# The last gate chunk and the final norm of a two-block transformer kernel in two halves, and four norms' sums spread by one product with ones

## The chip, the cores and the metric

One NeuronCore of a Trainium2 chip runs the whole kernel in one launch. The metric is the device time in microseconds (us); a time given for a kernel is the median of several executions.

## The reference, cut to what matters

Two transformer blocks over 512 positions of width 1024, in float32. The first has two kinds of attention and a gated feed-forward layer. The second has a pooling mixer, an attention, a second feed-forward layer, and then its last two steps, which are where most of the change lies:

```python
x = x + (silu(h @ w_ffn_gate) * (h @ w_ffn_up)) @ w_ffn_down      # h = rms_norm_2(x, norm_ffn)
gate = sigmoid(rms_norm_2(x, norm_ple) @ w_ple_gate)
x = x + gate * (p @ w_ple_proj)
return rms_norm_2(x, norm_final)

def rms_norm_2(x, gain):
    inv = rsqrt(mean(x * x, axis=-1) + 1e-6)
    return x * inv * gain
```

`rms_norm` of the first block is the same formula.

## The kernel before, in words

Everything is held transposed: `X` has 8 chunks (KD) of 128 features on the partitions, with the 512 positions along the row. A matrix product of one output chunk of 128 features is a *group*: for each of the 8 input chunks three products of 128x128 weights with 128x512 inputs (high part times high part, high times low, low times high), 24 in all, that add up in one bank of the accumulator `ps` (`three`, `group`). Weights come in units of two chunks through three slots. SyncE (SP) loads a unit when the unit three before it is used up (`load`), ScalarE (ACT) rounds it to `w_hi`, VectorE (DVE) subtracts to get `w_lo` (the two functions called `split`). Each engine's order is written out by hand, and an engine that waits for a semaphore holds up all that stands behind it.

**A "late" norm.** Four norms are not applied to a product's input, but to its output: `n_ffn_pre` (before feed-forward ff1), `n_mix2` (before in2), `n_ffn2` (before ff2) and `n_ple` (before the gate, pleg). While the products already run on the unnormed input, ACT squares the 8 chunks of `X` (`square`), GpSimd (POOL) adds the first seven squares into `sqsum` (`sum_squares`, L408), and TensorE (PE) sums `sqsum` and the eighth square over the partitions: `total` has 8 small products, one per 128 positions and source, each of them two instructions of one column (16 in all), and gives 4 sums on each partition. DVE makes the variance of them (`variance`), ACT a guess by Ln and Exp (`guess`), DVE refines it and writes four 128x128 diagonal matrices (`factors`), PE multiplies those with a matrix of ones (`factor`, two instructions of 512 columns), so that all partitions hold the 512 factors, and ACT copies them to `factors_sb` (`late_factors`). From then on DVE scales each group's bank by `factors_sb` as it takes it out (`scaled`, L1226). Banks 0 to 3 take the groups in turn, so that a group waits until the bank's last one has been taken out (`wait_bank`); in ff1 and in2 groups 4 and 5 go to two other banks.

In ff1 and in2 ("wide") the first four groups run interleaved by input chunk (`first_units`), `total` stands ahead of the seventh input chunk and `factor` behind the eighth. In ff2 and pleg only the first two groups are interleaved, `total` follows them, and `factor` follows the next group.

**The end.** pleg has 8 groups. DVE's loop over j takes group j+1 out (`gate_in`, scaled into `hf`), waits for ACT's sigmoid of group j, multiplies by `PP` and adds to `X` (two tensor_tensor). So the additions of chunk 6 stand behind `gate_in(7)`, which waits for the last group. ACT squares each finished chunk for the final norm and POOL adds up. Then, one after the other: `total(n_final)`, `variance`, `guess` (ahead of it a table load, L850), `factors`, `factor`, eight scalar_tensor_tensor from `X` to `OUT` (L1233) and eight stores of 256 KB by SP (L394).

Lines of the helpers, which the trace names: L464 every product, L835 every activation, L1226 tensor_tensor, L1229 and L1230 tensor_scalar, L1233 scalar_tensor_tensor, L404 and L408 POOL's clearing and adding, L375 weight loads.

Of the kernel before, what the change touches and what calls it, by code (L numbers as in the profile page):

```python
# [10 lines left out]
D = 1024  # L11
S = 512
# [75 lines left out]
def build(nc, xT, pT, weights, gains, consts, outT):  # L88
# [10 lines left out]
    with ctx:  # L99
# [105 lines left out]
        with ExitStack() as st:  # L205
# [40 lines left out]
            sem(n) for n in ("silu_ready", "prod_ready", "prod_hi_ready", "prod_lo_ready"))  # L246
        out_ready, out_stored = sem("out_ready"), sem("out_stored")
# [23 lines left out]
        class Norm:  # L271
# [7 lines left out]
            def __init__(self, n, kind, before):  # L279
# [4 lines left out]
                n_f32 = {"split": n, "late": 1, "added": n, "final": 0}[kind]  # L284
                self.factor_used = self.f32(n_f32)
                for e in NORM_EVENTS:
                    norm_counts[e] += (n if e in ("squares", "summed") else n_f32 if e == "f32" else
                                       (n if kind in ("split", "late") else 0) if e in ("hi", "lo") else 1)

        norms = []  # L290
        for n, kind in ((KD, "late"), (4, "split"), (4, "split"), (KD, "added"), (KD, "late"), (KD, "added"),
                        (KD, "late"), (KD, "late"), (KD, "late"), (KD, "final")):
            norms.append(Norm(n, kind, norms[-1] if norms else None))
# [52 lines left out]

        def gcol(name, k):
            c = GAIN_AT[name] + k
            return gain[:, c:c + 1]


        X_PARTS = [(0, 1), (1, 2), (2, 4), (4, 6), (6, 8)]

# [13 lines left out]
        def _(sp):  # L367
# [27 lines left out]
            sp.wait_ge(out_stored, 16 * KD)  # L395
# [3 lines left out]
        def _(pool):  # L399
            def sum_squares(nm):  # L400
# [4 lines left out]
                for j in range(nm.n - 1):  # L405
# [56 lines left out]
        def _(pe):  # L462
# [58 lines left out]
            def total(nm):  # L521
# [8 lines left out]
                last.then_inc(nm.total.sem, 1)  # L530

# [196 lines left out]
            first_units("in2", U_IN2, 2, KS, h_hi, h_lo, parts_of(n_mix2.lo), {KD - 2: lambda: total(n_mix2)})  # L728
            factor(n_mix2)
# [87 lines left out]
            total(n_ple)  # L817
            for u in range(1, 4):
                unit("pleg", U_PLEG + u, 2 * u, 2, KS, h_hi, h_lo, after=lambda j: factor(n_ple) if j == 2 else None)
# [875 lines left out]
```

## Time and profile before

| | |
|---|---|
| time, median of 3 executions | 1394.39 us (1391.86 to 1395.15) |
| the profiled execution: its own time, its span | 1398.8 us, 1396.3 us |
| mean granted TensorE clock | 0.983 of full speed |
| busy share of the span: PE, DVE, ACT, POOL | 96%, 50%, 39%, 10% |
| chain of work that ended last: PE, DVE | 88%, 8% |

Start times in the rows are us from the start of the span. The columns of each view are named with the first group of rows that shows it. Products are pipelined: a row's duration is that of one product, but the next one starts before it ends, so the distance between starts is what one costs.

### The profile page before, as it was taken

Reading aid. Unit: us, or ns where it says so; the run is one execution under the profiler, and the core shown is the slowest. Engines: PE = TensorE matmul, PEld = TensorE weight load, DVE = VectorE, ACT = ScalarE, POOL = GpSimd, SP = SyncE. Lnnn points to the kernel's source line nnn. Section 1 sums busy time; section 2 is a strip of 40 time slices with the busy share of each in tenths; the row PEclk is TensorE's granted clock in tenths of the full one; section 3 lists DMA queues with packets and bytes.
Section 4 is the critical chain, followed back from the end, with each engine's and each line's share of the span. In section 5 each row is a group of like instructions: output and inputs, shape, how many; then the busy total and the mean of one; then the engine's idle time right before and its main releaser. Section 6 shows DMA issues by size and latency. Waiting matters only on the chain.

```text
span 1396.3 us, 14839 instructions
## 1 busy us (share of the span) xinstructions
PE 1341.4 (96%) x6120; PEld 1076.3 (77%) x6120; DVE 691.5 (50%) x922; ACT 544.8 (39%) x736; POOL 144.8 (10%) x132
## 2 busy tenths in 40 slices
PE   7987989999999999998999999999999999999995
PEld 5764658788888888886888888788888888888874
DVE  6998864644453442216434445664444453423254
ACT  6458864532232332224224555542332232322232
POOL 3441002500000000012000001011000000010011
PEclk9999989999999999998999999999999999999997
DMA  6110003122222323231322111223232222232311
GB/s 238 61 60 2 0 1 121 61 77 104 91 91 94 111 69 102 85 113 67 103 93 83 61 61 61 91 91 98 87 111 97 91 91 94 79 104 95 111 61 60
DMA packets 20595, 117.75 MB, mean 84 GB/s; under 512 B 2480, under 2 KB 2864, under 8 KB 9904
## 3 DMA queue, kind: packets, MB, share of 16 engines
q1 hardware_dynamic: 19392, 114.57, 24.0%
q10 hardware_dynamic: 1136, 2.24, 0.4%
q8 instruction: 48, 0.79, 0.2%
q14 instruction: 19, 0.16, 0.0%
HBM read 114.70 MB, written 2.10 MB: 84 GB/s over the span
## 4 chain that ended last, share of the span: by engine, by line
PE 88%; DVE 8%; DMA 1%; ACT 1%; issue 1%; SPq 0%; POOL 0%; POOLq 0%; DVEq 0%
PE ps L464 87%; PE ps L660 2%; DVE rt L1233 1%; DVE w_lo L1226 1%; DMA X<-x_t 1%; DVE nmax L1388 1%; DVE F L1230 1%; DVE X L1226 0%; ACT w_hi L835 0%; DVE rt L1226 0%; DVE ps L1233 0%; DMA w_raw<-weights 0%; DVE OUT L1233 0%; DVE h_lo L1233 0%; DVE y L1226 0%
## 5 line engine op out<-in xcount | busy, mean ns | idle before, releaser
L464 PE MATMUL ps<-h_hi,w_hi 128*128 128x512 f32 x1248 | 497.1, 398 | 19.6 <-DVE w_lo L1226 11.3
L464 PE MATMUL ps<-h_lo,w_hi 128*128 128x512 f32 x1248 | 488.8, 392 | 0.0
L464 PE MATMUL ps<-h_hi,w_lo 128*128 128x512 f32 x1248 | 488.6, 392 | 0.0
L1226 DVE TENSOR_TENSOR w_lo<-w_raw,w_hi 128x2048 fp32r<-128x2048 f32 (+2 forms) x117 | 247.6, 2119 | 276.0 <-ACT w_hi L835 275.9
L464 PEld LDWEIGHTS ps<-h_hi,w_hi 128*128 128x128 f32 x1248 | 236.0, 189 | 78.8 <-issue 14.3
L835 ACT ACTIVATE w_hi<-w_raw 128x2048 fp32r<-128x2048 f32 (+2 forms) x117 | 201.2, 1721 | 196.7 <-DMA w_raw<-weights 196.5
L464 PEld LDWEIGHTS ps<-h_lo,w_hi 128*128 128x128 f32 x1248 | 236.0, 189 | 51.1 <-issue 3.1
L464 PEld LDWEIGHTS ps<-h_hi,w_lo 128*128 128x128 f32 x1248 | 235.9, 189 | 49.7
L408 POOL TENSOR_TENSOR sqsum<-sqsum,sq 128x512 f32<-128x512 f32 x62 | 90.0, 1452 | 901.8 <-ACT sq L835 900.1
L1226 DVE TENSOR_TENSOR hf<-ps,factors_sb 128x512 f32<-128x512 f32 x56 | 38.6, 691 | 199.4 <-PE ps L464 194.3
L464 PE MATMUL ps<-mid_lo,w_hi 128*128 128x512 f32 x352 | 136.9, 389 | 0.0
L464 PE MATMUL ps<-mid_hi,w_hi 128*128 128x512 f32 x352 | 136.9, 389 | 0.0
L464 PE MATMUL ps<-mid_hi,w_lo 128*128 128x512 f32 x352 | 136.9, 389 | 0.0
L835 ACT ACTIVATE mid_hi<-hf 128x512 fp32r<-128x512 f32 x44 | 27.8, 633 | 209.9 <-DVE hf L1226 209.9
L464 PEld LDWEIGHTS ps<-mid_hi,w_hi 128*128 128x128 f32 x352 | 66.1, 188 | 13.8
L464 PEld LDWEIGHTS ps<-mid_hi,w_lo 128*128 128x128 f32 x352 | 66.1, 188 | 13.7
L464 PEld LDWEIGHTS ps<-mid_lo,w_hi 128*128 128x128 f32 x352 | 66.1, 188 | 13.6
L835 ACT ACTIVATE sq<-sq 128x512 f32<-128x512 f32 x44 | 27.7, 632 | 87.9 <-DVE sq L1226 87.9
L660 PEld LDWEIGHTS ps<-ident,F 128*128 128x128 f32 x208 | 23.9, 147 | 42.7 <-DVE F L1230 40.4
L835 ACT ACTIVATE sq<-X 128x512 f32<-128x512 f32 x48 | 30.2, 629 | 64.1 <-DVE X L1226 63.2
L660 PE MATMUL ps<-ident,F 128*128 128x128 f32 x208 | 37.4, 296 | 15.2 <-DVE F L1230 15.2
L1388 DVE TENSOR_REDUCE nmax<-ps 128x1 f32<-128x512 f32 (+2 forms) x64 | 37.5, 587 | 18.0 <-PE ps L464 17.9
(178 smaller groups left out, 1198.1 us busy)
## 6 DMA issues: line engine op xcount, KB each, us to landing
w_raw<-weights SPq DMA_DIRECT2D x81, 1024.0 KB, 4.8
w_raw<-weights SPq DMA_DIRECT2D x32, 704.0 KB, 4.2
out_t<-OUT SPq DMA_DIRECT2D x8, 256.0 KB, 2.0
X<-x_t SPq DMA_DIRECT2D x3, 512.0 KB, 7.4
c<-constants ACTq DMA_DIRECT2D x1, 1280.0 KB, 9.2
w_raw<-weights SPq DMA_DIRECT2D x4, 256.0 KB, 7.6
wp_raw<-weights SPq DMA_DIRECT2D x1, 1024.0 KB, 6.8
X<-x_t SPq DMA_DIRECT2D x2, 256.0 KB, 4.0
```

The costliest lines, as they stand in the source:

```text
L408: nc.gpsimd.tensor_tensor(sqsum[:, :], sqsum[:, :], sq[:, j % 2, :], ALU.add).then_inc(nm.summed.sem, 1)
L464: return nc.tensor.matmul(out, lhsT, rhs, start=start, stop=stop, skip_group_check=loose)
L660: last = nc.tensor.transpose(ps[:, 3 + s % 2, (kb - k0) * P:(kb - k0 + 1) * P], prob[:, s % 3, (kb - k0) * P:(kb - k0 + 1) * P], ident[:, :])
L835: return nc.scalar.activation(out, in_, func, **kw)
L1226: return nc.vector.tensor_tensor(out, a, b, op)
L1230: else nc.vector.tensor_scalar(out, a, s1, None, op0))
L1233: return nc.vector.scalar_tensor_tensor(out=out, in0=a, scalar=s, in1=b, op0=op0, op1=op1)
L1388: nc.vector.tensor_reduce(nmax[:, s:s + 1], ps[:, s % 3, at:end], AX.X, ALU.max, negate=True).then_inc(nmax_ready, 1)
```

## The change

It has two parts.

**Sums spread by one product.** The four late norms get the kind "wide". POOL adds all eight squares (nine events in place of eight), and PE multiplies a 128x128 matrix of ones with `sqsum`: one product of 512 columns (two instructions), after which every partition holds all 512 sums. `total` and `factor` are not called for these norms. DVE and ACT then work on 128x512 tiles: one tensor_scalar out of the bank, Ln and Exp, two tensor_tensor and one scalar_tensor_tensor that writes `factors_sb`. The product stands ahead of the eighth input chunk in ff1 and in2, and in ff2 and pleg three input chunks into group 2.

**The last group and the final norm in halves.** Group 7 of pleg runs as two runs of 24 products of 256 columns, into banks 3 and 6. DVE's loop ends with chunk 6, whose additions no longer stand behind a `gate_in(7)`. Taking out, sigmoid, additions, square, sums, variance, guess, diagonals, the product with ones and the writing of `OUT` are done by halves of 256 positions. Sixteen scalar_tensor_tensor of 256 columns take the place of eight of 512. Six stores take the place of eight; their rows in memory are 1 KB in place of 2 KB, and ACT issues one of them.

The diff, cut to its core:

```diff
+        STORES = [(0, 0, 4), (0, 4, 8), (1, 0, 3), (1, 3, 5), (1, 5, 7), (1, 7, 8)]
...
-            for k in range(KD):
-                sp.wait_ge(out_ready, k + 1)
-                sp.dma_start(outT[k * P:(k + 1) * P, :], OUT[:, k, :]).then_inc(out_stored, 16)
+            for n, (i, k0, k1) in enumerate(STORES):
+                if n != len(STORES) - 2:
+                    sp.wait_ge(out_ready, KD * i + k1)
+                    sp.dma_start(*store(i, k0, k1)).then_inc(out_stored, 16)
...
+            def wide_total(nm):
+                pe.wait_ge(*nm.summed(nm.sums))
+                mm(ps[:, nm.ss_bank, :], ones[:, :], sqsum[:, :]).then_inc(nm.total.sem, 1)
...
                 if wide:
-                    first_units(phase, u_ff, 2, KS, h_hi, h_lo, parts_of(nm.lo), {KD - 2: lambda: total(nm)})
-                    factor(nm)
+                    first_units(phase, u_ff, 2, KS, h_hi, h_lo, parts_of(nm.lo), {KD - 1: lambda: wide_total(nm)})
                 else:
                     first_units(phase, u_ff, 1, KS, h_hi, h_lo, parts_of(nm.lo))
-                    total(nm)
-                    unit(phase, u_ff + 1, 2, 2, KS, h_hi, h_lo, after=lambda j: factor(nm) if j == 2 else None)
+                    unit(phase, u_ff + 1, 2, 2, KS, h_hi, h_lo, hooks={2: {3: lambda: wide_total(nm)}})
...
-            total(n_final)
-            factor(n_final)
+            for i in range(2):
+                bank = ps[:, GATE_BANKS[i], half_of(i)]
+                for k in KS:
+                    t = slice((KD + k) * P, (KD + k + 1) * P)
+                    mm(bank, w_hi[slot][:, t], h_hi[:, k, half_of(i)], k == 0, False)
+                    mm(bank, w_hi[slot][:, t], h_lo[:, k, half_of(i)], False, False)
+                    last = mm(bank, w_lo[slot][:, t], h_hi[:, k, half_of(i)], False, k == KD - 1)
+                last.then_inc(half_done, 1)
+            sums, square = sqsum[:, :], sq[:, 1, :]
+            pe.wait_ge(*n_final.summed(KD))
+            final_part(0, sums)
+            final_part(1, sums)
+            for i in range(2):
+                pe.wait_ge(*n_final.squares(KD + i))
+                final_part(i, square).then_inc(n_final.total.sem, 1)
+            final_factor(0)
+            final_factor(1)
...
+            def wide_guess(nm):
+                act.wait_ge(*nm.var(1))
+                link(af(hf[:, 1, :], hf[:, 0, :], ACT.Ln, scale=-2.0))
+                af(hf[:, 1, :], hf[:, 1, :], ACT.Exp, scale=-0.5).then_inc(nm.guess.sem, 1)
...
+            square(n_final, KD - 2, X[:, KD - 2, :])
+            half_gate(0)
+            half_square(0)
+            half_gate(1)
             tables(LN_EXP)
-            guess(n_final)
+            half_square(1)
+            half_guess(0)
+            half_guess(1)
+            i, k0, k1 = STORES[-2]
+            act.wait_ge(out_ready, KD * i + k1)
+            act.dma_start(*store(i, k0, k1)).then_inc(out_stored, 16)
...
+            def wide_factors(nm):
+                dve.wait_ge(*nm.total(1))
+                ts(hf[:, 0, :], ps[:, nm.ss_bank, :], -0.5 / D, ALU.mult, -0.5 * EPS, ALU.add).then_inc(nm.var.sem, 1)
+                dve.wait_ge(*nm.guess(1))
+                link(tt(hf[:, 0, :], hf[:, 0, :], hf[:, 1, :], ALU.mult))
+                link(tt(hf[:, 0, :], hf[:, 0, :], hf[:, 1, :], ALU.mult))
+                stt(factors_sb[:, :], hf[:, 0, :], 1.5, hf[:, 1, :], ALU.add, ALU.mult).then_inc(nm.f32.sem, 1)
...
-            for j in range(KD):
-                if j + 1 < KD:
+            for j in range(KD - 1):
+                if j + 1 < KD - 1:
                     gate_in(j + 1)
...
+            for i in range(2):
+                half_gate_in(i)
+                half_gate_out(i)
+            half_variance(0)
+            half_variance(1)
+            half_factors(0)
+            half_factors(1)
+            half_apply(0, 0, KD)
+            half_apply(1, 0, KD)
```

The new functions of which only calls are shown do to 256 columns what their namesakes do to 512; `final_part` is two of the small products of `total`, `final_factor` a product of ones with two of the diagonal matrices.

## Rows read from the trace of the kernel before

**Rows 1.** The page: busy time of the engines, and the chain that ended last by engine.
```profile
PE 1341.4 (96%) x6120; PEld 1076.3 (77%) x6120; DVE 691.5 (50%) x922; ACT 544.8 (39%) x736; POOL 144.8 (10%) x132
PE 88%; DVE 8%; DMA 1%; ACT 1%; issue 1%; SPq 0%; POOL 0%; POOLq 0%; DVEq 0%
```

**Rows 2.** Timeline of PE in pleg: start, duration, operation, count, idle before and releaser.
```profile
1339.20 0.39 PE L464 MATMUL ps<-h_hi,w_lo 128*128 128x512 f32 x1
1339.43 0.95 PE L464 MATMUL ps<-ones,sqsum 128*128 128x1 f32 x8
...
1341.13 0.49 PE L464 MATMUL ps<-h_hi,w_hi 128*128 128x512 f32 x1
...
1346.72 1.02 PE L464 MATMUL ps<-diag,ones 128*128 128x512 f32 x2
1347.17 0.80 PE L464 MATMUL ps<-h_hi,w_hi 128*128 128x512 f32 x1
1347.81 0.40 PE L464 MATMUL ps<-h_lo,w_hi 128*128 128x512 f32 x1
...
1353.95 0.50 PE L464 MATMUL ps<-h_hi,w_hi 128*128 128x512 f32 x1 [0.72 <-DVE w_lo L1226]
```

**Rows 3.** Timeline of ACT, then of DVE, in the same stretch.
```profile
1329.08 0.63 ACT L835 ACTIVATE sq<-X 128x512 f32<-128x512 f32 x1 [3.00 <-DVE X L1226]
...
1347.77 0.60 ACT L835 ACTIVATE factors_sb<-ps 128x512 f32<-128x512 f32 x1 [4.53 <-PE ps L464]
...
1348.41 1.29 DVE L1226 TENSOR_TENSOR hf<-ps,factors_sb 128x512 f32<-128x512 f32 x2 [4.96 <-ACT factors_sb L835]
```

**Rows 4.** Timeline of PE in ff2, where group 3 ends and group 4 begins.
```profile
988.54 0.39 PE L464 MATMUL ps<-h_hi,w_lo 128*128 128x512 f32 x1
989.01 0.47 PE L464 MATMUL ps<-h_hi,w_hi 128*128 128x512 f32 x1
```

**Rows 5.** Groups of DVE by form: line, operation, count | busy, mean ns | idle before.
```profile
L1226 DVE TENSOR_TENSOR hf<-ps,factors_sb 128x512 f32<-128x512 f32 x56 | 38.6, 691 | 199.4 <-PE ps L464 194.3 <-ACT factors_sb L835 5.0
...
L1388 DVE TENSOR_REDUCE nmax<-ps 128x1 f32<-128x512 f32 x32 | 21.9, 686 | 6.5 <-PE ps L464 6.5
...
L1388 DVE TENSOR_REDUCE nmax<-ps 128x1 f32<-128x257 f32 x16 | 6.7, 421 | 3.9 <-PE ps L464 3.7
```

**Rows 6.** Timeline of PE in the attention of block 2: products of 128 to 512 columns.
```profile
754.89 1.49 PE L464 MATMUL ps<-E_hi,c 128*128 128x512 f32 x10
756.22 1.56 PE L464 MATMUL ps<-E_lo,c 128*128 128x512 f32 x10
```

**Rows 7.** Weight loads (PEld) by form.
```profile
L464 PEld LDWEIGHTS ps<-h_hi,w_hi 128*128 128x128 f32 x1248 | 236.0, 189 | 78.8 <-issue 14.3 <-DVE h_lo L1233 6.2 <-ACT PP L835 3.8
```

**Rows 8.** Timeline of PE at the end, then the table load of ACT.
```profile
1375.62 0.39 PE L464 MATMUL ps<-h_hi,w_lo 128*128 128x512 f32 x1
1380.56 1.87 PE L464 MATMUL ps<-ones,sqsum 128*128 128x1 f32 x8 [4.56 <-POOL sqsum L408]
...
1386.37 2.08 PE L464 MATMUL ps<-diag,ones 128*128 128x512 f32 x2 [2.23 <-DVE diag L1230]
...
1380.07 1.28 ACT L850 ACT_TABLE_LOAD   x1
```

**Rows 9.** Windows of the end: stretch, length, busy (count) by engine, granted clock, DMA.
```profile
1380.50:1384.20 3.70, 3.57 (x16) 3.49 (x16) 0.03 (x1) 0.85 (x1) 0.01 (x1) 0.50 0.00 0
```

**Rows 10.** Timeline of DVE, and one row of POOL, in the last part of pleg.
```profile
1357.74 1.67 DVE L1226 TENSOR_TENSOR X<-X,hf 128x512 f32<-128x512 f32 x1
...
1388.48 5.36 DVE L1233 SCALAR_TENSOR_TENSOR OUT<-X,gain,ps 128x512 f32<-128x512 f32 x8 [2.17 <-PE ps L464]
...
1357.56 1.30 POOL L408 TENSOR_TENSOR sqsum<-sqsum,sq 128x512 f32<-128x512 f32 x1 [2.52 <-ACT sq L835]
```

**Rows 11.** DMA queues: packets, MB, share of 16 engines; 1380 to 1397, then 630 to 650.
```profile
q1 hardware_dynamic: 1152, 2.10, 31.9%
...
q10 hardware_dynamic: 288, 0.23, 3.6%
```

More of the change, by code:

```diff
@@ L352, in build, with store @@
         X_PARTS = [(0, 1), (1, 2), (2, 4), (4, 6), (6, 8)]
+        STORES = [(0, 0, 4), (0, 4, 8), (1, 0, 3), (1, 3, 5), (1, 5, 7), (1, 7, 8)]
+        def store(i, k0, k1):
+            return (outT[k0 * P:k1 * P, half_of(i)].rearrange("(k p) s -> p k s", p=P), OUT[:, k0:k1, half_of(i)])
         def landed(u):
@@ L404, in sum_squares @@
                 nc.gpsimd.memset(sqsum[:, :], 0.0).then_inc(nm.summed.sem, 1)
-                for j in range(nm.n - 1):
+                for j in range(nm.sums - 1):
                     pool.wait_ge(*nm.squares(j + 1))
@@ L726, in vee @@
                 last.then_inc(v2tr_done, 1)
[L728 to L729 removed]
+            first_units("in2", U_IN2, 2, KS, h_hi, h_lo, parts_of(n_mix2.lo), {KD - 1: lambda: wide_total(n_mix2)})
             for u in range(2, 8):
@@ L816, in _, with final_part, final_factor @@
             first_units("pleg", U_PLEG, 1, KS, h_hi, h_lo, parts_of(n_ple.lo))
-            total(n_ple)
             for u in range(1, 4):
-                unit("pleg", U_PLEG + u, 2 * u, 2, KS, h_hi, h_lo, after=lambda j: factor(n_ple) if j == 2 else None)
-            total(n_final)
-            factor(n_final)
+                unit("pleg", U_PLEG + u, 2 * u, 2 if u < 3 else 1, KS, h_hi, h_lo,
+                     hooks={2: {3: lambda: wide_total(n_ple)}})
+            def final_part(i, src):
+                for b in (2 * i, 2 * i + 1):
+                    last = mm(ps[:, SUM_BANKS[i], b:b + 1], src[:, b * P:(b + 1) * P], ones[:, 0:1],
+                              src is sums and b == 2 * i, True, loose=True)
+                return last
+            def final_factor(i):
+                pe.wait_ge(*n_final.diag(i + 1))
+                mm(ps[:, FACTOR_BANKS[i], 0:HALF], ones[:, :], diag[:, 2 * i:2 * i + 2, :]).then_inc(n_final.factor.sem, 1)
+            slot = (U_PLEG + 3) % SLOTS
+            wait_bank("pleg", 7)
+            pe.wait_ge(evac_dve, EVAC["pleg", 4][1])
+            for i in range(2):
[15 more added lines that the diff above has]
+            final_factor(1)
         @block.scalar
@@ L1425, in ffn @@
             def ffn(phase, u_ff, mids0, nm, wide):
-                variance(nm)
-                factors(nm)
-                dve.wait_ge(*nm.f32(1))
+                wide_factors(nm)
                 for i in range(KF // 2):
@@ L1456, in _ @@
             apply_post(n_ffn_post, F, "norm_ffn_post", KD, n_mix2, "norm_mix_2", U_IN2 + 2)
-            variance(n_mix2)
-            factors(n_mix2)
+            wide_factors(n_mix2)
             def chunk2(j):
@@ L1566, in _ @@
             late_low(n_ple, "norm_ple_2", KD - 1)
-            variance(n_ple)
-            factors(n_ple)
-            dve.wait_ge(*n_ple.f32(1))
+            wide_factors(n_ple)
             def gate_in(j):
@@ L1583, in _, with half_gate_in @@
                 tt(X[:, j, :], X[:, j, :], hf[:, j % 2, :], ALU.add).then_inc(x_new[1], 1)
+            gate_in(0)
+            for j in range(KD - 1):
+                if j + 1 < KD - 1:
+                    gate_in(j + 1)
+                gate_out(j)
                 if j < 4 and j % 2 == 0:
                     split(U_PLEG + j // 2 + 2)
-            variance(n_final)
-            factors(n_final)
-            dve.wait_ge(*n_final.factor(1))
-            for k in range(KD):
-                stt(OUT[:, k, :], X[:, k, :], gcol("norm_final_2", k), ps[:, R_BANK, :], ALU.mult, ALU.mult
-                    ).then_inc(out_ready, 1)
+            def half_gate_in(i):
+                dve.wait_ge(half_done, i + 1)
+                tt(hf[:, 1, half_of(i)], ps[:, GATE_BANKS[i], half_of(i)], factors_sb[:, half_of(i)], ALU.mult
+                   ).then_inc(half_in, 1)
@@ new lines, in half_factors, with half_apply @@
+            def half_factors(i):
+                b = slice(2 * i, 2 * i + 2)
+                dve.wait_ge(*n_final.guess(i + 1))
+                link(refine(stat[:, 3, b], stat[:, 0, b], stat[:, 2, b]))
+                for c in (2 * i, 2 * i + 1):
+                    last = ts(diag[:, c, :], ident[:, :], stat[:, 3, c:c + 1], ALU.mult)
+                last.then_inc(n_final.diag.sem, 1)
+            def half_apply(i, k0, k1):
+                dve.wait_ge(*n_final.factor(i + 1))
+                for k in range(k0, k1):
+                    stt(OUT[:, k, half_of(i)], X[:, k, half_of(i)], gcol("norm_final_2", k),
+                        ps[:, FACTOR_BANKS[i], 0:HALF], ALU.mult, ALU.mult).then_inc(out_ready, 1)
```

66 lines of the change are left out of this document (43 added, 23 removed).

## The prediction

> **What bounds the kernel now.** I read the page first: PE is busy for 96% of the span and holds 88% of the chain that ended last [rows 1]. So away from the end a change is worth what it takes off PE's own queue, or off a wait of PE. The timeline of PE through one late norm, in pleg, shows what the norm costs there: the sixteen small products begin at 1339.43 and the next ordinary product at 1341.13, and between 1346.72 and 1347.81 the factor product stands with one ordinary one [rows 2]. Then the timelines of ACT and DVE: the first group is taken out at 1348.41, as soon as ACT has copied the factors [rows 3], and PE waits 0.72 us ahead of group 4, since the weights' low part stands on DVE and ACT behind that take-out [rows 2]. Last the end: PE's last group ends at 1376.01 (1375.62 + 0.39), and the remaining 20.3 us of the span are one chain that passes from engine to engine, in which PE works at the 0.50 granted clock, its 1.2 GHz level [rows 8, 9].
>
> **The norms' sums.** Removed on PE, per norm: the small products, 1341.13 - 1339.43 = 1.70 us, and the factor product. An ordinary product costs 0.23 (1339.20 to 1339.43), so the factor product costs 1347.81 - 1346.72 - 0.23 = 0.86 [rows 2]. Added: one product of ones with 512 columns, the same shape, 0.86. What is left is 1.70 us per norm.
> - ff1 and in2: PE runs without a wait around the norm, and the gain is PE's: 1.70 each, 3.40.
> - ff2: 1.70, and group 4 no longer waits for its bank. That wait is 989.01 - 988.54 - 0.23 = 0.24 [rows 4]. 1.94.
> - pleg: here the chain to the first take-out counts, since PE waits for what stands behind it. Before, it takes from 1339.43 to 1348.41, 8.98 us. After: nine products of group 2 (9 x 0.23 = 2.07), the product up to its result (1.05, as from 1346.72 to ACT's 1347.77 [rows 2, 3]), one DVE step of 512 columns (0.69 [rows 5]), Ln and Exp (2 x 0.63 [rows 3]), three DVE steps (3 x 0.69), 0.1 for handing over: 7.24. The take-out comes 1.74 earlier, PE itself is 1.70 earlier, so the wait of 0.72 stays and the gain is 1.70.
>
> Sum 3.40 + 1.94 + 1.70 = **7.0 us**. The five wide steps of DVE and ACT and POOL's eighth addition cost nothing in ff1, in2 and ff2: two to four groups of 24 x 0.23 = 5.5 us each cover them. Without that cover they would cost what they cost in pleg.
>
> The added wait: PE's queue now waits inside a group for POOL's last addition, and all products stand behind it. In pleg the last square starts at 1329.08 [rows 3] and POOL needs 1.30 for an addition [rows 10], so the sum is there before 1332; PE comes to it at 1341.5. In ff1, in2 and ff2 the squares also end groups ahead of the product. On DVE the first take-out, on ACT the table load and the next weights' split wait behind the chain; all are earlier than before. SP's load of the small weight tile in in2 waits for the norm's sum, which comes up to 12 products (2.8 us) later, but it stands behind a load that waits for PE's first group anyway: nothing.
>
> **The end, on the axis of the profile.** First the half products. Whole ones cost 0.23, half of it is 0.115. The nearest row is a run of ten products with 2560 columns in 756.22 - 754.89 = 1.33 us, 0.133 for a mean of 256 columns, but with four of 128 in it [rows 6]. I take 0.115: 48 x 0.115 = 5.5, as the whole group, with a bound of 48 x 0.133 = 6.4, 0.9 more. So half 1 ends at 1376.0.
> - DVE's take-out, sigmoid, table load, square of half 1. A step of 256 columns: 257 in place of 512 columns save 686 - 421 = 265 ns [rows 5], so 0.69 becomes 0.43; I take 0.43 for ACT too. The table load is 1.28 [rows 8] and covers the two additions. 3 x 0.43 + 1.28 = 2.57: 1378.6. Half 0's additions stand ahead on DVE and may meet POOL's last addition: one of 512 columns took 1.67 in place of 0.69 when POOL had begun 0.18 earlier [rows 10]. Between 0 and 1.0; I take the middle, 0.5: 1379.1. That the additions of chunk 6 no longer wait for the last group, and POOL with them, is what makes the sum of seven squares ready by then.
> - The sums: four small instructions are left in this place, at 1.87 / 8 = 0.23 each [rows 8], 0.9; at the full clock (0.95 / 8 [rows 2]) 0.5. I take 0.9, as the engine has little to do between: 1380.0.
> - Variance to diagonals: DVE writes both halves' diagonals before it applies anything, so the 2.23 of before stays [rows 8]: 1382.2. The first half's product with ones, 2.08 / 2, runs beside half 1's diagonals; 0.1 is left. 1382.3.
> - Sixteen steps of 256 columns: 5.36 / 8 - 0.265 = 0.405 each [rows 5, 10], 6.5 in place of 5.4: 1388.8.
> - From the last step to the end 1396.3 - (1388.48 + 5.36) = 2.46, kept; a smaller last store may save 0.3, more stores in rows of 1 KB may cost 0.3.
>
> DVE's last step ends at 1388.8 in place of 1393.84: **5.0 us**. Bounds: best 5.0 + 0.5 + 0.4 + 0.3 = 6.2; worst 5.0 - 0.5 - 0.9 - 0.3 = 3.3. ACT's own store is its last instruction and holds up nothing.
>
> The row of 257 columns shows 421 ns where half of 686 would be 343 [rows 5]. A rule speaks against halves here: the Trainium skill, "VectorE: DVE Perf Modes", section "The TRN2 errata — SBUF-src ops pay a fixed extra latency per instruction", says that a vector instruction pays a fixed latency however small it is, and advises tiles of 512 elements or more; by its formula for float32, an estimate, 256 elements take (256 + 151) / 0.96 = 424 ns. The trace agrees with that. With 424 ns for each of the sixteen steps the sum would be 0.3 us longer, 1382.7.
>
> Total 7.0 + 5.0 = 12.0. The durations are those of one execution (1398.8 us, of which the span is 1396.3), 4.4 us above the median of the runs. None of the steps scales with that, so I take 12.0 from the median: 1394.39 - 12.0 = **1382.4 us**.
>
> **The rivals.**
> - *Weight loads show under half products.* Each product has a load of 189 ns [rows 7]; under 512 columns it is hidden, since 0.23 is all that a pair costs [rows 2]. If a half product can't hide it, 48 x (0.189 - 0.115) = 3.6 us are lost: 1386.0. For: the load is longer than 0.115. Against: ten products with ten loads in 1.33 us [rows 6], less than 189 ns each. A rule of the Trainium skill ("TensorE: Matmul & The Clock Gate", "Part 3: Packing small matmuls — row/col tiling") would have it so, as it lets a load overlap a running product only in another group of rows; the rows of whole products disagree.
> - *The wide chain decides in ff2 and pleg.* If the five steps of 512 columns take 1.7 us longer than I add up, the gain there goes: 12.0 - 3.6 = 8.4, 1386.0. For: pleg has no slack, PE waits there before and after. Against: all its steps have rows.
> - *The end gives nothing.* More instructions with a fixed part, DVE and POOL in each other's way, half 0's factors behind half 1's variance in DVE's order, so that the halves hardly overlap (the change would then not do what it says): 1394.39 - 7.0 = 1387.4. With the rival above: 1391.0, within 0.3%.
> - *Slower: stores in rows of 1 KB.* 2.10 MB become 2048 rows, 128 per DMA engine. The first store can go four steps after 1382.3, at 1383.9, less the 7.0 of the norms: 1376.9. The end is not earlier than before if 128 rows take over 1396.3 - 2.46 - 1376.9 = 16.9 us, so from 132 ns a row. Before, a packet takes 0.319 x 16 x 17 us / 1152 = 75 ns; those of 0.8 KB on average at 630 to 650 take 0.036 x 16 x 20 / 288 = 40 ns [rows 11]. At 180 ns the time would be 1400.5. It needs more than twice a 2 KB row for 1 KB.
>
> **How the numbers follow.** Forecast 0.61; loads shown 0.08; wide chain 0.12; end gives nothing 0.10; both of these 0.05; stores 0.04. A measurement of this kernel can tell about 0.3%, 4.2 us, from no change: faster 0.61 + 0.08 + 0.12 + 0.10 = 0.91, same 0.05, slower 0.04. The forecast's own bounds are 1381.2 to 1384.1, and with the runs' half spread of 1.65 some 1379.5 to 1385.8; the first two rivals lie at 1386.0. From 1379 to 1387 holds these three, 0.81.
>
> **What would show it.** In the changed profile: one pair of products `ones, sqsum` of 512 columns per norm and 1.7 us less between the products around it; no idle of PE in ff2, 0.7 ahead of pleg's group 4; half products 0.115 apart; the table load between sigmoid and square of half 1; `OUT` steps 0.4 apart, the first some 6.3 us after PE's last gate product; the last store landing 2.5 after the last step. Wrong would be: PE waiting at the product with ones, half products 0.19 apart, or DMA still busy long after DVE's last step.

## The result and the profile after

The changed kernel takes 1383.18 us (median of 5 executions, 1382.63 to 1386.45) against 1394.39 for the kernel before on the same chip: a ratio of 0.9919 [0.9899, 0.9938], 11.2 us less. The prediction was 1382.4 in a range of 1379 to 1387. The profiled execution took 1383.08 with a span of 1381.4, 14.9 us under the span of before; why that is more than the medians differ by is told below.

**The sums.** PE's timeline in pleg after the change, which answers to [rows 2]:

```profile
1332.18 0.39 PE L481 MATMUL ps<-h_hi,w_lo 128*128 128x512 f32 x1
1332.40 1.02 PE L481 MATMUL ps<-sqsum,ones 128*128 128x512 f32 x2
1332.86 0.80 PE L481 MATMUL ps<-h_hi,w_hi 128*128 128x512 f32 x1
1333.50 0.40 PE L481 MATMUL ps<-h_lo,w_hi 128*128 128x512 f32 x1
...
1343.24 0.50 PE L481 MATMUL ps<-h_hi,w_hi 128*128 128x512 f32 x1 [0.93 <-DVE w_lo L1297]
1343.58 0.39 PE L481 MATMUL ps<-h_lo,w_hi 128*128 128x512 f32 x1
```

The sixteen small products and the factor product are gone. One pair of 512 columns stands in their place, and it costs 1333.50 - 1332.40 - 0.23 = 0.87 us, what the factor product cost (0.86). The products run through without a wait for the sum, and PE still waits ahead of group 4 for the weights' low part, 0.93 in place of 0.72. What follows in the chain is seen in DVE's timeline, with two rows of ACT's behind it (they answer to [rows 3]):

```profile
1333.46 0.69 DVE L1300 TENSOR_SCALAR hf<-ps 128x512 f32<-128x512 f32 x1 [10.85 <-PE ps L481]
1335.52 1.42 DVE L1297 TENSOR_TENSOR hf<-hf 128x512 f32<-128x512 f32 x2 [1.36 <-ACT hf L883]
1336.97 0.69 DVE L1304 SCALAR_TENSOR_TENSOR factors_sb<-hf 128x512 f32<-128x512 f32 x1
1337.70 1.29 DVE L1297 TENSOR_TENSOR hf<-ps,factors_sb 128x512 f32<-128x512 f32 x2
...
1334.19 1.30 ACT L883 ACTIVATE hf<-hf 128x512 f32<-128x512 f32 x2 [12.89 <-DVE hf L1300]
1335.50 1.28 ACT L898 ACT_TABLE_LOAD   x1
```

From PE's pair to the first take-out 1337.70 - 1332.40 = 5.30 us pass. The take-out comes 1348.41 - 1337.70 = 10.71 before that of [rows 3].

How far each product stands ahead of the same product of before, stage by stage, tells where the gain arose. In ff1 I take the last product ahead of `total` in the kernel before and the second one behind its factor product; 25 others lie between these two in either kernel. The timeline of PE in ff1, before:

```profile
291.68 0.39 PE L464 MATMUL ps<-h_hi,w_lo 128*128 128x512 f32 x1
291.91 0.28 PE L464 MATMUL ps<-ones,sqsum 128*128 128x1 f32 x2
...
299.20 1.02 PE L464 MATMUL ps<-diag,ones 128*128 128x512 f32 x2
299.65 0.80 PE L464 MATMUL ps<-h_hi,w_hi 128*128 128x512 f32 x1
300.29 0.40 PE L464 MATMUL ps<-h_lo,w_hi 128*128 128x512 f32 x1
```

and the same two products and what stands between them, after:

```profile
287.74 0.39 PE L481 MATMUL ps<-h_hi,w_lo 128*128 128x512 f32 x1
...
290.69 1.02 PE L481 MATMUL ps<-sqsum,ones 128*128 128x512 f32 x2
...
294.54 0.39 PE L481 MATMUL ps<-h_lo,w_hi 128*128 128x512 f32 x1
```

300.29 - 291.68 = 8.61 became 294.54 - 287.74 = 6.80: **1.81** us. The same reading gives, over the whole trace:

| up to | ahead of before, us | of it new |
|---|---|---|
| start of ff1 | 1.5 | 1.5, ahead of any edit |
| ff1, ahead of the norm | 3.9 | 2.4, clock |
| ff1, behind the norm | 5.7 | 1.8, norm |
| in2, behind the norm | 6.6 | -1.0, clock; 1.8, norm |
| ff2, behind group 4 | 8.8 | 2.2, norm and the bank's wait |
| pleg, ahead of the norm | 9.1 | 0.3, weights that landed sooner |
| pleg, group 4 | 10.7 | 1.6, norm |
| end | 14.9 | 4.2 |

The norms gave 1.8, 1.8, 2.2 and 1.6, which is 7.5 before rounding, and the end 4.2, 11.7 in all. The other 3.2 lie where the two kernels are the same. (In in2 the granted clock fell sooner and came back later in the changed kernel's profile than in that of before.) Windows over the start of ff1 (stretch, length, busy and count by engine, granted clock, DMA) show the largest of them, before:

```profile
273.00:276.00 3.00, 2.25 (x5) 1.39 (x6) 2.97 (x6) 2.37 (x5) 1.51 (x2) 0.57 0.00 0
276.00:280.00 4.00, 4.00 (x11) 3.03 (x11) 2.77 (x4) 3.19 (x4) 1.28 (x1) 0.50 0.01 4
```

and after:

```profile
273.00:276.00 3.00, 2.45 (x11) 2.03 (x12) 2.93 (x6) 1.87 (x5) 2.05 (x2) 1.00 0.02 5
276.00:280.00 4.00, 4.00 (x19) 3.33 (x18) 2.82 (x3) 2.92 (x3) 1.30 (x1) 1.00 0.00 0
```

At 0.50, the 1.2 GHz level, eleven products ran in four microseconds, at 1.00 nineteen. So the profiles differ by 14.9, and the medians by 11.2, near the 11.7 that the edits account for.

**The end.** PE's timeline from the first half product on, which answers to [rows 8]:

```profile
1359.70 0.28 PE L481 MATMUL ps<-h_hi,w_hi 128*128 128x256 f32 x1
...
1365.33 0.28 PE L481 MATMUL ps<-h_hi,w_lo 128*128 128x256 f32 x1
1365.88 1.05 PE L481 MATMUL ps<-ones,sqsum 128*128 128x1 f32 x8 [0.28 <-POOL sqsum L425]
1366.80 0.58 PE L481 MATMUL ps<-ones,sq 128*128 128x1 f32 x4
1368.68 1.01 PE L481 MATMUL ps<-ones,sq 128*128 128x1 f32 x4 [1.29 <-ACT sq L883]
1370.92 2.20 PE L481 MATMUL ps<-diag,ones 128*128 128x256 f32 x4 [1.23 <-DVE diag L1301]
```

The 48 half products lie 5.63 / 47 = 0.12 apart. PE's wait for POOL, 4.56 us before, is 0.28; the wait for the diagonals, 2.23, is 1.23, since the first half's product goes while DVE writes the second half's. On DVE, POOL and ACT, one after the other (for [rows 10] and the table load of [rows 8]):

```profile
1364.72 1.39 DVE L1297 TENSOR_TENSOR X<-X,hf 128x256 f32<-128x256 f32 x1
1366.03 0.41 DVE L1297 TENSOR_TENSOR hf<-ps,factors_sb 128x256 f32<-128x256 f32 x1
...
1372.18 6.36 DVE L1304 SCALAR_TENSOR_TENSOR OUT<-X,gain,ps 128x256 f32<-128x256 f32 x16 [0.33 <-PE ps L481]
...
1362.66 3.17 POOL L425 TENSOR_TENSOR sqsum<-sqsum,sq 128x512 f32<-128x512 f32 x2 [3.96 <-ACT sq L883]
...
1366.91 1.28 ACT L898 ACT_TABLE_LOAD   x1
1368.21 0.42 ACT L883 ACTIVATE sq<-X 128x256 f32<-128x256 f32 x1
```

Half 0's addition takes 1.39 where that of half 1 takes 0.42; half 1's square waits for ACT's table load. The scaling starts at 1372.18 and ends at 1378.54, and the span ends 2.8 later, at 1381.35. Windows of one microsecond (the last two figures are the DMA engines' busy share and GB/s) say what binds there:

```profile
1373.00:1374.00 1.00, 0.12 (x1) 0.00 (x0) 1.00 (x4) 0.00 (x0) 0.00 (x0) 0.50 0.00 0
1374.00:1375.00 1.00, 0.00 (x0) 0.00 (x0) 1.00 (x4) 0.00 (x0) 0.00 (x0) 0.50 0.18 65
1375.00:1376.00 1.00, 0.00 (x0) 0.00 (x0) 1.00 (x4) 0.00 (x0) 0.00 (x0) 0.50 1.08 385
1376.00:1377.00 1.00, 0.00 (x0) 0.00 (x0) 1.00 (x4) 0.00 (x0) 0.00 (x0) 0.50 0.87 307
...
1379.00:1380.00 1.00, 0.00 (x0) 0.00 (x0) 0.00 (x0) 0.00 (x0) 0.00 (x0) 0.50 1.09 385
```

The DMA engines stand idle until 1374.8, for the first store waits for four steps. From then on they move 382 to 387 GB/s in each whole window up to 1380, but for 307 in that from 1376 to 1377.

### The profile page after: what moved, and what is told of

Read it like the earlier page. It is cut to its first block, busy times and chain, and to the rows that moved or that the text cites. A ratio compares the mean times of both kernels' runs of the same rounds, so it can differ in the third digit from the quotient of the medians.

```text
span 1381.4 us, 14763 instructions
## 1 busy us (share of the span) xinstructions
PE 1329.6 (96%) x6082; PEld 1067.1 (77%) x6082; DVE 701.1 (51%) x921; ACT 546.1 (40%) x736; POOL 149.5 (11%) x136
## 4 chain that ended last, share of the span: by engine, by line
PE 87%; DVE 9%; DMA 1%; ACT 1%; issue 1%; POOL 0%; SPq 0%; DVEq 0%; POOLq 0%
PE ps L481 86%; PE ps L682 2%; DMA w_raw<-weights 1%; DVE rt L1304 1%; DVE w_lo L1297 1%; DVE nmax L1469 1%; DVE F L1301 1%; DVE X L1297 1%; ACT w_hi L883 1%; DVE OUT L1304 0%; DVE rt L1297 0%; DVE hf L1297 0%; DVE ps L1304 0%; POOL sqsum L425 0%; DVE h_lo L1304 0%
## 5 line engine op out<-in xcount | busy, mean ns | idle before, releaser
L481 PE MATMUL ps<-h_hi,w_hi 128*128 128x512 f32 (+1 forms) x1256 | 497.1, 396 | 20.1 <-DVE w_lo L1297 11.7
L481 PE MATMUL ps<-h_lo,w_hi 128*128 128x512 f32 (+1 forms) x1256 | 489.1, 389 | 0.0
L481 PE MATMUL ps<-h_hi,w_lo 128*128 128x512 f32 (+1 forms) x1256 | 488.9, 389 | 0.0
L481 PEld LDWEIGHTS ps<-h_hi,w_hi 128*128 128x128 f32 x1256 | 236.9, 189 | 78.3 <-issue 14.1
L425 POOL TENSOR_TENSOR sqsum<-sqsum,sq 128x512 f32<-128x512 f32 x66 | 94.8, 1436 | 910.0 <-ACT sq L883 908.2
L1297 DVE TENSOR_TENSOR hf<-ps,factors_sb 128x512 f32<-128x512 f32 (+1 forms) x57 | 38.7, 681 | 190.5 <-PE ps L481 190.4
L481 PEld LDWEIGHTS ps<-mid_lo,w_hi 128*128 128x128 f32 x352 | 66.1, 188 | 13.8
L481 PEld LDWEIGHTS ps<-mid_hi,w_hi 128*128 128x128 f32 x352 | 66.1, 188 | 13.8
L883 ACT ACTIVATE sq<-X 128x512 f32<-128x512 f32 (+1 forms) x49 | 30.4, 620 | 68.2 <-DVE X L1297 67.2
```

The source lines that it names most:

```text
L425: nc.gpsimd.tensor_tensor(sqsum[:, :], sqsum[:, :], sq[:, j % 2, :], ALU.add).then_inc(nm.summed.sem, 1)
L481: return nc.tensor.matmul(out, lhsT, rhs, start=start, stop=stop, skip_group_check=loose)
L883: return nc.scalar.activation(out, in_, func, **kw)
L1297: return nc.vector.tensor_tensor(out, a, b, op)
```

## The experiments

The measure of the end is the **stretch** from the start of PE's last gate product to the end of the span, from the trace's own times: 20.7 before, 16.0 after. Of this difference of 4.7, 0.4 is no gain, since the last half product starts 0.4 later than a whole one would (48 halves take 0.3 longer than 24 whole ones, and the last half starts 0.1 closer to the end). That leaves the 4.2 of the table. The changed kernel, run twice more as it is, gave 1384.72 us, 0.9918 [0.99, 0.9935], and 1383.81 us, 0.993 [0.9916, 0.9944], so the medians of equal kernels differ by up to 1.5 us; the stretch was 16.0 in all three profiles. One thing can move it: the granted clock under PE's small sums, by 0.3 to 0.4 in two cases below. Ratios are to the kernel before on the same chip.

**1. The parts, each alone.** The first run has the four wide norms and before's end (all hunks of the end undone, of which one stands here):

```diff
-                unit("pleg", U_PLEG + u, 2 * u, 2 if u < 3 else 1, KS, h_hi, h_lo,
-                     hooks={2: {3: lambda: wide_total(n_ple)}})
...
+                unit("pleg", U_PLEG + u, 2 * u, 2, KS, h_hi, h_lo, hooks={2: {3: lambda: wide_total(n_ple)}})
+            total(n_final)
+            factor(n_final)
```

The second has the end in halves and before's norms (the start of its diff); the third is the changed kernel again.

```diff
-        for n, kind in ((KD, "late"), (4, "split"), (4, "split"), (KD, "added"), (KD, "wide"), (KD, "added"),
-                        (KD, "wide"), (KD, "wide"), (KD, "wide"), (KD, "final")):
+        for n, kind in ((KD, "late"), (4, "split"), (4, "split"), (KD, "added"), (KD, "late"), (KD, "added"),
+                        (KD, "late"), (KD, "late"), (KD, "late"), (KD, "final")):
...
```

> The four wide norms alone, with the end as before. If the norms' sums give what the prediction added up (7.0 us, 7.6 by the shifts read from the two traces), the time is about 1387 us, ratio 0.995, and the stretch from PE's last gate product to the end of the span stays 20.7 us. If the gain came from the end alone, or from the chance differences between the two profiled executions (1.5 us ahead of ff1, 2.4 us of half clock at the start of ff1), it stays within 2 us of before.

> The halves at the end alone, with the four norms as before. If the end gives 4 to 5 us by itself, the time is about 1390 us, ratio 0.997, and the stretch from PE's last gate product to the end of the span is 16.1 us as in the changed kernel. If the end gains only together with the norms, the stretch is over 18 us.

> The changed kernel itself, on the chip of the others: ratio 0.992, stretch from PE's last gate product to the end 16.1 us. If the half clock at the start of ff1 or in2 comes and goes by chance, its profile may show it in another place than before.

The norms alone took 1389.54 us, 0.9945 [0.9927, 0.9964], which is 7.7 us less (5.0 to 10.2), with a stretch of 20.4. The end alone took 1391.77 us, 0.9966 [0.9952, 0.998], 4.7 us less (2.8 to 6.7), with a stretch of 16.0. The two ratios make 0.9911 together, and the changed kernel has 0.9918. The traces say the same more sharply: read as in the table, the run of the norms alone has 1.8, 1.8, 2.2 and 1.6 at the four norms, 7.5 in all, and the run of the end alone has 0.0 there. So the parts don't disturb each other, and each is as large as the trace of the changed kernel says. That the stretch of the norms alone is 0.3 under the 20.7 of before is mostly the clock: its first eight small sums took 1.61 at a mean granted clock of 0.60, those of before 1.87 at 0.50 [rows 8, 9].

**2. Order or halves.** The end has two changes in one: additions and squares of chunk 6 are no longer behind the last group, and the last group's own chain runs in halves. This run has wide norms and before's end, with only DVE's order moved.

```diff
-                if j + 1 < KD:
+                if j + 1 < KD - 1:
                     gate_in(j + 1)
+                if j == KD - 1:
+                    gate_in(j)
```

> The wide norms, and at the end no halves at all: only DVE's order is changed, so that the additions of chunk 6 stand ahead of taking out group 7. Theory A, that halving makes the end's gain: the stretch from PE's last gate product to the end falls only by the 0.45 us by which POOL was later than the eighth square, to 20.2 us, time 1386.7. Theory B, that the order makes most of it, since POOL's last addition, the first eight small products and the last chunk's additions all come earlier: stretch 17.5 to 18.2 us, time 1384 to 1385.

The run took 1386.54 us, 0.9931 [0.9915, 0.9948], and its stretch of 18.7 lies between the two theories. The rows of DVE, POOL, PE and ACT in this run say why:

```profile
1369.13 1.65 DVE L1241 TENSOR_TENSOR X<-X,hf 128x512 f32<-128x512 f32 x1
...
1368.97 1.26 POOL L424 TENSOR_TENSOR sqsum<-sqsum,sq 128x512 f32<-128x512 f32 x1 [2.90 <-ACT sq L852]
...
1370.28 1.05 PE L480 MATMUL ps<-ones,sqsum 128*128 128x1 f32 x8 [3.30 <-POOL sqsum L424]
...
1368.28 0.61 ACT L852 ACTIVATE sq<-X 128x512 f32<-128x512 f32 x1
```

DVE had added chunk 6 in time, but ACT squared it only behind the last group's sigmoid. So POOL's addition still came late, and held DVE's addition and PE's sums. A second run moved ACT's square too:

```diff
+                if j == KD - 1:
+                    act.wait_ge(x_new[1], j)
+                    square(n_final, j - 1, X[:, j - 1, :])
                 act.wait_ge(evac_dve, EVAC["pleg", j][1])
...
-                if j:
+                if 0 < j < KD - 1:
```

> As the run with the order alone (wide norms, whole last group, whole end, DVE adds chunk 6 before it takes group 7 out), and ACT squares chunk 6 ahead of the sigmoid of group 7 too, as the changed kernel does. Theory A (the part of the end's gain that the order alone doesn't give is the halves' own): POOL's last addition is already free of the chain there, and the stretch from the start of PE's last gate product to the end stays at 18.7 within 0.3. Theory B (the order alone was only half done, since ACT's square of chunk 6 stood behind the last sigmoid, at 1368.28, so that POOL's addition came at 1368.97, clashed with DVE's last addition, 1.65 in place of 0.69, and held PE's sums): POOL is done before PE's last product ends, DVE's last addition falls to 0.7, and the stretch comes to 17.5 to 17.9, so that the order on both engines gives some 2.8 us of the end's gain and the halves 1.6 to 1.8.

The run took 1386.5 us, 0.9932 [0.9915, 0.9949]; its stretch, 1365.52 to 1383.4, is 17.9, the upper edge of B. PE's wait for POOL shrinks and DVE's addition takes its usual 0.69 again, in PE's and DVE's timelines:

```profile
1366.48 1.05 PE L480 MATMUL ps<-ones,sqsum 128*128 128x1 f32 x8 [0.57 <-POOL sqsum L424]
...
1368.06 0.69 DVE L1244 TENSOR_TENSOR X<-X,hf 128x512 f32<-128x512 f32 x1
```

So of the end's gain of 4.2 the order on both engines is worth 20.37 - 17.93 = 2.4 us, all that is done in halves 17.93 - 16.02 - 0.42 = 1.5, and the 0.3 that is left is mostly the clock under before's small sums. Theory B had put the order at 2.8, since it counted from 20.7.

**3. What of the halves counts.** Four edits of the changed kernel. *Whole last group*: 24 products of 512 columns, then halves as before.

```diff
-            for i in range(2):
-                bank = ps[:, GATE_BANKS[i], half_of(i)]
+            bank = ps[:, GATE_BANKS[0], :]
...
-                last.then_inc(half_done, 1)
+            last.then_inc(half_done, 2)
```

> The changed kernel, but gate group 7 is 24 products of 512 columns in one bank again, and both halves of the rest start behind its last one; all else is in halves. Theory A (what halving the products gives is that half 0's take-out, sigmoid and addition lie beside half 1's products): PE's products take as long as before (24 at about 0.23, 5.5 us, against 5.75 for 48 halves), half 0's 2.5 us of work come behind them, and the stretch from the start of the last product to the end grows from 16.0 by 1.2 to 2.2 us. Theory B (half 1's chain behind the table load sets the end, and half 0 only waits for it): it grows by under 0.6 us.

The run took 1385.74 us, 0.9936 [0.9922, 0.9949]; its stretch, 1366.97 to 1384.4, is 17.5 and 1.4 longer, theory A. Its last product starts 0.4 sooner, though: from the wide product to the last product it is 32.5 us, where the changed kernel has 32.9. So half products, which let half 0's steps run beside PE, are worth 1.0 net.

*Whole scaling*: both factor products into one bank, eight steps of 512 columns, eight stores of 2 KB rows.

```diff
-            half_apply(0, 0, KD)
-            half_apply(1, 0, KD)
+            dve.wait_ge(*n_final.factor(2))
+            for k in range(KD):
+                stt(OUT[:, k, :], X[:, k, :], gcol("norm_final_2", k), ps[:, FACTOR_BANKS[0], :], ALU.mult, ALU.mult
+                    ).then_inc(out_ready, 1)
...
```

> The changed kernel, but the two factor products write the halves of one bank and the last scaling runs over 512 positions: 8 steps and 8 stores of 2 KB rows, as before the change. Theory A (the halves of the output are worth nothing: the transfers bind the stretch behind the last scaling in either form, 9.22 us from its start to the end with halves, 7.82 without): the scaling starts about 1.0 later, behind the second half's product, and ends as far behind its start as in the kernel before, so the span stays within 0.5 us of the changed kernel's 1381.4 to 1382.2. Theory B (the early start of the first half's stores is what the end gains): the stretch from the start of PE's last half product to the end, 16.0 to 16.1 us with halves, grows by over 1.0 us. Time by A: 1383 to 1385, by B: 1386 and more.

The run took 1384.52 us, 0.993 [0.9918, 0.9942]; its stretch, 1365.79 to 1381.4, is 15.6 and 0.4 shorter. So the output in halves, with its six stores, gains nothing and costs 0.4. The scaling starts 1.0 later, at 1373.61, but takes 5.36 in place of 6.36, and its stores go after one step each, so that the transfers start 9.5 behind the last half product in both kernels (DVE's timeline, then windows):

```profile
1373.61 5.36 DVE L1301 SCALAR_TENSOR_TENSOR OUT<-X,gain,ps 128x512 f32<-128x512 f32 x8 [1.31 <-PE ps L480]
...
1375.00:1376.00 1.00, 0.00 (x0) 0.00 (x0) 1.00 (x3) 0.00 (x0) 0.00 (x0) 0.50 0.75 291
1376.00:1377.00 1.00, 0.00 (x0) 0.00 (x0) 1.00 (x3) 0.00 (x0) 0.00 (x0) 0.50 1.05 408
```

*Ten finer stores*: the first after one step.

```diff
-        STORES = [(0, 0, 4), (0, 4, 8), (1, 0, 3), (1, 3, 5), (1, 5, 7), (1, 7, 8)]
+        STORES = [(0, 0, 1), (0, 1, 2), (0, 2, 4), (0, 4, 6), (0, 6, 8), (1, 0, 2), (1, 2, 4), (1, 4, 6), (1, 6, 7), (1, 7, 8)]
```

> The changed kernel with ten stores instead of six: the first two of one chunk of 128 rows each, the rest of two, the last two of one. Theory A (the transfers bind the end and start too late: the first of the six stores waits for four scaling steps, 1.7 us): the DMA queues start about 1.2 us sooner behind the first step, the end comes 0.4 to 1.0 us sooner, the stretch from PE's last half product 15.0 to 15.6. Theory B (the stores run as fast as the scaling steps come, and ten issues cost more than six): no change within 0.3 us, or up to 0.5 us later.

The run took 1382.72 us, 0.9918 [0.9904, 0.9932]; its stretch, 1362.97 to 1378.6, is 15.65 and 0.4 shorter, just short of theory A's range. That is as much as whole scaling gave, with the halves kept. So it isn't shown that the halves themselves cost anything: the run before changed steps, rows and stores at once, and finer stores alone win the 0.4 too. The scaling of this run starts at 1369.81, and DMA is busy from 1371 on, though not full, since the sixteen steps now set the pace:

```profile
1371.00:1372.00 1.00, 0.00 (x0) 0.00 (x0) 1.00 (x4) 0.00 (x0) 0.00 (x0) 0.50 0.70 247
1372.00:1373.00 1.00, 0.00 (x0) 0.00 (x0) 1.00 (x4) 0.00 (x0) 0.00 (x0) 0.50 0.66 234
```

*PE sums the seventh square itself*, four products more and one addition of POOL less.

```diff
-            pe.wait_ge(*n_final.summed(KD))
-            final_part(0, sums)
-            final_part(1, sums)
+            pe.wait_ge(*n_final.summed(KD - 1))
+            pe.wait_ge(*n_final.squares(KD - 1))
+            for src in (sums, seventh):
+                final_part(0, src)
+                final_part(1, src)
```

> The changed kernel, but PE takes the seventh square into the sums itself with four more products, and POOL's last addition is gone. Theory A (POOL's addition of 3.17 for two holds DVE's first half addition, 1.39 instead of about 0.43, and PE's sums, 0.28): the first half addition comes down to 0.4 to 0.5, the sums start without a wait on POOL, and the stretch from PE's last half product to the end falls from 16.0 by 0.5 to 0.9 us, the time to about 1384. Theory B (the stretch is set from half 1's chain, behind the table load and its square, and by the stores): the addition gets shorter, and the end doesn't move (16.0 within 0.2).

The run took 1384.28 us, 0.9928 [0.9915, 0.9941]; its stretch, 1365.82 to 1381.5, is 15.65 and 0.4 shorter, between the two theories. POOL's clash is real, as DVE's and then POOL's timeline of this run show:

```profile
1365.20 0.43 DVE L1299 TENSOR_TENSOR X<-X,hf 128x256 f32<-128x256 f32 x1
...
1363.14 1.74 POOL L425 TENSOR_TENSOR sqsum<-sqsum,sq 128x512 f32<-128x512 f32 x1 [3.96 <-ACT sq L885]
```

The addition fell from 1.39 to 0.43, but only 0.4 of that reached the end; half 1's take-out then waits for PE, and its square for the table load. The medians of these four can't be told from the changed kernel's; their stretches, of one profile each, are what the verdicts rest on. The last four small sums took 1.01 to 1.02 us in all four, as in the changed kernel, so the clock has no part in these differences.

**4. The wait in pleg, and all together.** *Early splitting*: ACT and DVE split the weights of groups 4 and 5 before the norm's wide chain, while they wait for PE's sum.

```diff
+            split(U_PLEG + 2)
             wide_guess(n_ple)
...
-                if j < 4 and j % 2 == 0:
-                    split(U_PLEG + j // 2 + 2)
+                if j == 2:
+                    split(U_PLEG + 3)
```

> The changed kernel, but ACT and DVE split the weights of gate groups 4 and 5 into high and low parts ahead of the gate norm's wide chain, in the time in which they wait for PE's sum, instead of behind the first gate chunk. Theory A (with the gate norm shorter, the low half of those weights is now what PE's group 4 waits for, 0.93 us): the wait goes, PE starts group 4 behind group 3 without a gap, and all that follows is 0.9 sooner; ACT's 1.90 and DVE's 2.29 us of splitting no longer stand between the first gate chunks either. The stretch from the wide sum's product (1332.40) to the start of the last half product (1365.33), 32.9 us, comes to 32.0. Theory B (another wait takes its place, the bank that DVE takes out late): it stays over 32.6.

The run took 1382.08 us, 0.9917 [0.9903, 0.9931]. From the wide product at 1333.03 to the last half product at 1364.72 it is 31.7 us in place of 32.9, theory A. The 1.2 is more than the 0.93 of the wait: a product else starts 0.16 before the one ahead of it ends (0.39 long, 0.23 apart), and the second one behind the idle time started 0.34 later and not 0.23 (1343.24 and 1343.58 after the change). The stretch fell too, from 16.0 to 15.6, and that is the clock: the last four small sums took 0.61 us at a granted clock of 1.00, where the changed kernel's three profiles have 1.01 at 0.50. Whether the splitting has a part in that isn't shown. DVE's row has moved into the time in which it stood idle (a row of PE with the four sums behind it):

```profile
1325.18 2.29 DVE L1298 TENSOR_TENSOR w_lo<-w_raw,w_hi 128x2048 fp32r<-128x2048 f32 x1 [1.98 <-ACT w_hi L883]
...
1368.08 0.61 PE L481 MATMUL ps<-ones,sq 128*128 128x1 f32 x4 [1.29 <-ACT sq L883]
```

*All that helped*: early splitting; PE's seventh square; half 0 summed, refined and spread first; half 1's square on DVE; three chunks scaled in halves and five whole; nine stores. The core of it:

```diff
+            tt(sq[:, 1, h], X[:, KD - 1, h], X[:, KD - 1, h], ALU.mult).then_inc(n_final.squares.sem, 1)
             half_variance(0)
...
+            half_apply(0, 0, LEAD)
+            dve.wait_ge(*n_final.factor(2))
+            for k in range(LEAD, KD):
+                stt(OUT[:, k, :] ... ps[:, 0:5:4, 0:HALF], ALU.mult, ALU.mult).then_inc(out_ready, 1)
+            half_apply(1, 0, LEAD)
```

> All that the runs so far found, together: the early splitting; PE sums the seventh square; half 0 is summed first and its factors are made ahead of half 1's; DVE squares half 1 itself, so that it doesn't wait behind ACT's table load; the first three chunks are scaled in halves of 256 (half 0 first, half 1 last) and the other five over 512 positions, with nine smaller stores. Theory A (the links add up): 0.9 from the splitting; scaling starts 5.8 behind the start of the last half product instead of 6.85, takes 5.75 instead of 6.36, and the last store lands 2.4 behind it: a stretch of 14.0 instead of 16.0; in all 2.5 to 3.0 under the changed kernel on the same chip, a ratio to the kernel before of about 0.990. Theory B (the stores bind the stretch whatever starts them, 2.10 MB at 390 to 400 GB/s): the stretch doesn't come under 15.3, in all 1.5 or less.

> The changed kernel as it is, on the same chip as the two others: a ratio of 0.992 within 0.001, and a stretch of 16.0 to 16.1 us from the start of the last half product to the end.

The first of these two runs took 1380.02 us, 0.9902 [0.9886, 0.9917], against 1383.81 for the changed kernel on the same chip: 3.8 us less, somewhat more than A's 2.5 to 3.0. The stretch, 1366.18 to 1380.0, is 13.8 (A: 14.0), and 1334.49 to 1366.18 is 31.7 as in the run before, so the two profiles account for 2.2 + 1.2 = 3.4. DVE's scaling starts 5.6 behind the start of the last half product; the transfers start 1.4 behind that, and from 1374 to 1377 they run at 388 to 406 GB/s:

```profile
1371.78 5.74 DVE L1310 SCALAR_TENSOR_TENSOR OUT<-X,gain,ps 128x256 f32<-128x256 f32 x11
...
1374.00:1375.00 1.00, 0.00 (x0) 0.00 (x0) 1.00 (x3) 0.00 (x0) 0.00 (x0) 0.50 1.07 388
1375.00:1376.00 1.00, 0.00 (x0) 0.00 (x0) 1.00 (x3) 0.00 (x0) 0.00 (x0) 0.50 1.05 406
```

This version is faster than the kernel before, and by its median and its stretch faster than the changed one, though the intervals of these two ratios just touch.

## Why the prediction was right, point by point

- **The total, 12.0; measured 11.2 by the medians (8.6 to 14.1) and 11.7 by the trace.** That it came so near is in part luck: the sums gave 0.5 more than added up and the end 0.8 less, and the interval of the medians is wider than either.
- **The sums, 7.0; measured 7.5 in the trace and in that of the norms alone.** One pair of 512 columns costs what the factor product cost (0.87 against 0.86), as put. ff1 and in2 gave 1.8 each where 1.70 was added up, ff2 2.2 where it was 1.94, pleg 1.6 where it was 1.70. The 0.1 more in ff1 and in2 can be read behind the small products of before: the first ordinary product there takes 0.49 [rows 2], and in ff2 the next one starts 0.33 behind it (976.83 and 977.16), not 0.23.
- **pleg's wait** was to stay at 0.7 and became 0.93: the chain to the first take-out is 5.30 from the pair (forecast 1.05 + 0.69 + 1.26 + 2.07 + 0.1 = 5.17), and PE comes there 0.1 sooner than put. The wait was real time, as the early splitting shows.
- **The wide chain hidden in ff1, in2 and ff2**: PE has no wait there. The rival that it decides is out.
- **The added wait of PE for POOL's eighth addition**: none shows.
- **The end, 5.0; measured 4.2.** This is the term that was mis-sized. Half products: 48 x 0.12 = 5.75, not 5.5, 0.3 lost. From the last half product's end (1365.61) to the end of scaling 12.93 where 12.8 was added up: POOL's clash cost half 1's take-out 0.42, near the 0.5 put down, and the sixteen steps took 6.36, not 6.5. Behind the last step 2.8 and not 2.46, another 0.4: the forecast kept before's tail because it put the last step at the head of the chain. The windows show the transfers there instead: the stream of 2.10 MB starts 2.6 us into the scaling and runs at 382 to 387 GB/s, but for one window, up to 1380; finer stores took these 0.4 away. 0.3 + 0.13 + 0.4 = 0.8, the difference.
- **What made the end gain** was argued as halves and, in one sentence, as order. The runs show order 2.4 and halves 1.5. Of the halves the products are worth 1.0 net; scaling in halves, which the forecast counted on to start the last part early, gave nothing, and with six stores it lost 0.4.
- **Weight loads under half products**: the loads take 192 ns each, the products follow 0.12 apart all the same, so they are hidden here. The rule of the Trainium skill that was weighed ("TensorE: Matmul & The Clock Gate", "Part 3: Packing small matmuls — row/col tiling") does not describe these rows. PEld's groups in this stretch, of which one stands for three:

```profile
L481 PEld LDWEIGHTS ps<-h_hi,w_hi 128*128 128x128 f32 x16 | 3.1, 192 | 0.0
```

- **The step of 256 columns** was taken at 405 ns from a row of 257 and came at 6.36 / 16 = 398. The Trainium skill's formula ("VectorE: DVE Perf Modes", "The TRN2 errata — SBUF-src ops pay a fixed extra latency per instruction") gave an estimate of 424. Its advice against small tiles holds here for the engine's own time: sixteen halves take 1.0 longer than eight whole ones. For the end of the kernel it made no difference once the stores were finer (15.65 against 15.6).
- **Stores in rows of 1 KB** were the slower rival, from 132 ns a row on. They run at 382 to 387 GB/s, against 389 to 408 with rows of 2 KB in the run with whole scaling. At 385 GB/s on 16 engines a row takes 16 x 1024 / 385 = 43 ns.
- **The base.** 12.0 was taken from the median and not from the profiled execution. That was right: 2.4 us of the profiles' difference are the half clock at the start of ff1 that the profiled execution of before had and that of the change had not.

## What to carry to other kernels

Where a chain passes from engine to engine at the end, look first for work that stands behind the last step only by the order in which the engines' programs are written, on every engine that has a part in it: moving DVE alone gave two thirds of what moving DVE and ACT gave. Halves pay where they let an engine work beside another that still runs (products: 1.0 net). They gain nothing where the transfers bind the end (scaling, stores): there let the first stores go after one or two steps and not after four. And measure a gain of under 2 us by the stretch in which it arises, since equal kernels' medians differ by as much.

## What the runs showed of the hardware

- The granted clock at the start of ff1 was at its 1.2 GHz level in the profiles of three kernels (before, norms alone, DVE's order alone) and at 2.4 GHz in those of the other eleven, though all have the same code there. It costs 2.4 us when it comes. In the three microseconds ahead of the same product, which starts at 273.04 in the profile of before and 0.4 ahead of the fall there, PE was busy for 1.44 to 1.46 in all fourteen, so the rows don't say what decides.
- The same goes for the end: the last four small sums of the changed kernel's form ran at 0.50 and took 1.01 in its three profiles, and at 1.00 in 0.61 with early splitting, which is 0.4 us of the kernel's time.
- A VectorE addition of two tensors in SBUF took 1.0 longer while POOL added: 1.39 for 0.43, 1.65 for 0.69. Taking out of the accumulator, with one operand in SBUF, kept its 0.69 beside POOL (1365.94 in the run with the order on both engines, POOL busy from 1363.27 to 1366.43).
- Behind an idle of 0.93 us PE's first product took 0.50 and the next started 0.34 later, where 0.23 is usual, at a granted clock of 1.00 throughout. Without that idle time the products came 1.2 sooner, 0.3 more than it lasts.
